# The opening of a two-layer hybrid backbone kernel: conditioning by row tiles, first blocks in passes, and a new order of three queues

## The chip, the core and the metric

The kernel runs on one core of a Trainium2 chip. The metric is the device time of the kernel in microseconds (us), as the median of several runs; less is better. PE is the tensor engine, DVE the vector engine, ACT the scalar engine, POOL the GpSimd engine, and SP the engine whose queue issues the loads.

## The reference

Two layers of a backbone run over 640 tokens: 128 context tokens (prompt) and 512 latent tokens (sample), width 1024. What the opening of the kernel computes is the first steps of layer 0, cut here to what matters:

```python
def _rmsnorm(x, g):
    y = xf * lax.rsqrt(jnp.mean(xf * xf, axis=-1, keepdims=True) + EPS)
    return (y * g.astype(jnp.float32)).astype(x.dtype)

def _modulation(cond, ada_w, ada_b):
    m = jax.nn.silu(cond) @ ada_w + ada_b
    return jnp.split(m[:, None, :], 6, axis=-1)
...
    sh1, sc1, ga1, sh2, sc2, ga2 = _modulation(cond, ada_w, ada_b)
    h = _rmsnorm(x, g_pre_mix) * (1.0 + sc1) + sh1
    mixed, side = mixer(_split_proj(h, w_in))
    x = x + ga1 * _rmsnorm(mixed @ w_out, g_post_mix)
    h = _rmsnorm(x, g_pre_ffn) * (1.0 + sc2) + sh2
    x = x + ga2 * _rmsnorm(_conv_ffn(h, w_up, conv_w, conv_b, w_down), g_post_ffn)
```

There are two conditioning rows: one for the context, one for the sample. Before the first projection `h @ w_in` can start, the kernel needs the shift and scale of both (16 column groups of 128 of `ada_w`), the row scale of the norm, and the transposed tokens.

## The kernel before, in words

The tokens are five tiles of 128 (`NT = 5`; tile 0 is the context). Every large product is taken in three parts from operands split in a high and a low half: high by high, high by low, and low by high. The high half is an ACT copy (`split_hi` and `lead_high`), the low half a DVE subtraction (`split_lo` and `lead_low`). Weights come through four slots of `raw` in an order fixed by tables; each engine has its own queue, written out by hand, and semaphores tie the queues together.

The opening is written apart from the loops over the layers. It has these pieces:

- Conditioning. SP loads the two rows of 1024 numbers as one row `cond_row` (L550). PE spreads it to all partitions with four products of a 1-partition column of ones, 512 columns each, into banks 0 to 3 (L2481). ACT takes the silu of each bank (L770). The first two make the row of the context, `cond[:, 0]`, the other two the row of the sample, `cond[:, 1]`.
- Modulation columns. SP loads 16 column groups of `ada_w` into the eight buffers of `lead`, first eight (half 0: groups 8, 0, 9, 1, 10, 2, 11, 3) and then eight more (half 1: groups 12, 4, 13, 5, 14, 6, 15, 7) into the buffers that come free. Five of them are done by PE (`lead_columns`, L2120: 0 to 2 are groups 0, 1, 2, then groups 4 and 5), eleven by DVE (`lead_products`, L1743 and L1746, one instruction for each conditioning row: 0 to 4 belong to half 0, 5 to 10 to half 1). `lead_mod(h)` on DVE finishes half h.
- Norm. For each tile ACT takes the squares and the root (`lead_squares`, L783 and L785), DVE the reciprocal (`row_scale`, L1388), ACT the scaled tokens `xl` (`lead_scaled`, L1041).
- Tokens by half. `lead_transposes(h, tt)` on PE (L2131) transposes four of the eight column groups of tile tt; a modulation by DVE (L1780) or ACT (L1051) writes `tf`, ACT copies the high half `aT_hi` (L1061), DVE makes `aT_lo` (L1787).
- First block. `lead_block(h, tt)` on PE takes the 12 products of tile tt with half h of the first 512 output columns: two weight granules (q), two k each, three products for each k (`mm3`, L2087 to L2089). It begins with a wait for `aT_lo` of its tile. The blocks run in order (0,0) to (0,4) and (1,0) to (1,4); after them the loops over the layers begin.

The queue of each engine around this:

```python
            for tt in range(NT):
                lead_block(0, tt)
                if tt < 2:
                    lead_columns((3 + tt,))
                if tt + 2 < NT:
                    lead_transposes(0, tt + 2)
                else:
                    lead_transposes(1, tt + 2 - NT)
```

Of the kernel before, what the change touches and what calls it, by code (L numbers as in the profile page):

```python
# [24 lines left out]
P = 128  # L25
# [142 lines left out]
def build(nc, t):  # L168
    with ExitStack() as ctx:
# [84 lines left out]
        with ExitStack() as s:  # L254
            xn = sb("xn", [P, 2, D], F32, s)
            zt = sb("zt", [P, W], F32, s)
            sq = sb("sq", [P, D], F32, s)
            with ExitStack() as s2:
                tf = sb("tf", [P, 2, KD, P], F32, s2)
                lead = sb("lead", [P, KD, 1024], F32, s2)  # L260
                xl = sb("xl", [P, NT, D], F32, s2)
                cond_row = sb("cond_row", [1, 2 * D], F32, s2)
                ones = sb("ones", [1, P], F32, s2)
                cond_T = sb("cond_T", [P, KD, 2], F32, s2)
            with ExitStack() as s2:
                s_sum = sb("s_sum", [P, 3, HP, HZ], F32, s2)
            y_mix = sb("y_mix", [P, NT, W], F32, s)
            gb_mix = sb("gb_mix", [P, 2, D], F32, s)
            h_all = sb("h_all", [P, KD, TZ], F32, s)
# [175 lines left out]
        def in_bank(b, tt):  # L445
            return IN_BANKS[b][tt]
# [76 lines left out]
        def _(sp_):  # L523
# [26 lines left out]
            sp_.dma_start(cond_row[:], t["cond"]).then_inc(cond_in, 16)  # L550
# [214 lines left out]
        def _(act):  # L765
# [5 lines left out]
            act.wait_ge(primed, 1)  # L771

# [294 lines left out]
            lead_scaled(1)  # L1067
            lead_high(0, 0)
            split_hi(1, 0)
            lead_squares(2)  # L1070
# [278 lines left out]
        def _(dve):  # L1349
# [444 lines left out]
            row_scale(0, 1, 0)  # L1794
            lead_mod(0)
            lead_modulate(0, 0)
            split_lo(0, 0)
            lead_low(0, 0)
            lead_modulate(0, 1)
            split_lo(1, 0)  # L1800
            row_scale(0, 2, 0)
            lead_low(0, 1)
            lead_products(5)
            row_scale(0, 3, 0)
            lead_products(6)
            lead_products(7)
            lead_low(0, 2)
            row_scale(0, 4, 0)
            lead_products(8)
            lead_low(0, 3)  # L1810
            lead_products(9)
            lead_products(10)
            lead_low(0, 4)
# [270 lines left out]
        def _(pe):  # L2084
# [65 lines left out]
            def lead_block(h, tt):  # L2150

                pe.wait_ge(norm_lo, NT * h + tt + 1)
                for q in (2 * h, 2 * h + 1):
                    if tt == 0:
                        pe.wait_ge(*freed(stream_of(q), 0))
                    for kk in range(2):
                        k = 2 * q + kk
                        i_ = mm3(bank[in_bank(0, tt)][:], aT_hi[:, k, toks(tt)], aT_lo[:, k, toks(tt)],
                                 w_hi[:, q, kk * W:(kk + 1) * W], w_lo[:, q, kk * W:(kk + 1) * W],
                                 k == 0, k == KD - 1)  # L2160
                    if tt == NT - 1:
                        i_.then_inc(w_used, 1)
                if h and tt < NT - 1:
                    i_.then_inc(in_done, 1)
# [314 lines left out]
            pe.wait_ge(cond_in, 16)  # L2479
            for i in range(4):  # L2480
                pe.matmul(bank[i][:], ones[:], cond_row[:, i * W:(i + 1) * W], start=True, stop=True).then_inc(cond_rows, 1)  # L2481
# [3 lines left out]
            lead_transposes(0, 0)  # L2485
            lead_transposes(0, 1)
            for tt in range(NT):
                lead_block(0, tt)
                if tt < 2:
                    lead_columns((3 + tt,))  # L2490
                if tt + 2 < NT:
                    lead_transposes(0, tt + 2)
                else:
                    lead_transposes(1, tt + 2 - NT)
# [297 lines left out]
```

## Time and profile before

| what | value |
|---|---|
| median of 3 runs | 1602.45 us (1602.03 to 1604.36) |
| the profiled execution, first to last instruction (its span) | 1601.0 us |
| PE busy | 1575.8 us (98%) |
| DVE busy | 1275.6 us (80%) |
| ACT busy | 794.1 us (50%) |
| POOL busy | 379.2 us (24%) |
| PE's share of the chain that ended last | 84% |
| DVE's share of the chain that ended last | 7% |

The profile is of one execution. Its own time is given as its span, 1601.0 us; the runs' times also hold what lies before the first and after the last instruction, and the median is 1.45 us over the span. Busy time is the time in which an engine executed; the chain that ended last is followed back from the last instruction to whatever released each step.

### The profile page before, as it was taken

Reading aid. Unit: us, or ns where it says so; the run is one execution under the profiler, and the core shown is the slowest. Engines: PE = TensorE matmul, PEld = TensorE weight load, DVE = VectorE, ACT = ScalarE, POOL = GpSimd, SP = SyncE. Lnnn points to the kernel's source line nnn. Section 1 sums busy time; section 2 is a strip of 40 time slices with the busy share of each in tenths; the row PEclk is TensorE's granted clock in tenths of the full one; section 3 lists DMA queues with packets and bytes.
Section 4 is the critical chain, followed back from the end, with each engine's and each line's share of the span. In section 5 each row is a group of like instructions: output and inputs, shape, how many; then the busy total and the mean of one; then the engine's idle time right before and its main releaser. Section 6 shows DMA issues by size and latency. Waiting matters only on the chain.

```text
span 1601.0 us, 28310 instructions
## 1 busy us (share of the span) xinstructions
PE 1575.8 (98%) x9688; PEld 1389.2 (87%) x9688; DVE 1275.6 (80%) x2255; ACT 794.1 (50%) x1483; POOL 379.2 (24%) x302
## 2 busy tenths in 40 slices
PE   8999999999999999999999999999999999999998
PEld 6788898689999999888878889967899999998886
DVE  7876677968999999966669556987689999998575
ACT  5433235638655565533383323274766565563333
POOL 0031033001455455200000400700035455541000
PEclk9999999999999999999999999999999999999999
DMA  9343265361222222454414414736312222335451
GB/s 369 122 132 111 74 222 179 95 168 55 66 81 89 79 92 79 148 168 158 152 40 145 138 54 134 260 107 146 79 64 82 80 91 79 92 92 178 125 184 66
DMA packets 65494, 195.04 MB, mean 122 GB/s; under 512 B 15361, under 2 KB 16769, under 8 KB 65153
## 3 DMA queue, kind: packets, MB, share of 16 engines
q1 hardware_dynamic: 50114, 175.54, 35.1%
q10 hardware_dynamic: 15296, 18.39, 3.5%
q8 instruction: 53, 0.87, 0.3%
q14 instruction: 31, 0.25, 0.1%
HBM read 187.05 MB, written 6.85 MB: 121 GB/s over the span
## 4 chain that ended last, share of the span: by engine, by line
PE 84%; DVE 7%; issue 2%; ACT 2%; DMA 1%; ACTq 1%; DVEq 0%; SPq 0%
PE bank L2087 14%; PE bank L2088 13%; PE bank L2089 13%; PE bank L2597 10%; PE bank L2599 10%; PE bank L2598 10%; DMA raw<-in_stream 1%; PE bank L2393 1%; PE bank L2457 1%; PE bank L2455 1%; PE bank L2453 1%; PE bank L2380 1%; PE bank L2109 1%; DVE w_lo L1354 1%; PE bank L2277 1%
## 5 line engine op out<-in xcount | busy, mean ns | idle before, releaser
L778 ACT ACTIVATE w_hi<-raw 128x1024 fp32r<-128x1024 f32 (+1 forms) x120 | 123.1, 1029 | 389.0 <-PE bank L2089 325.1
L1354 DVE TENSOR_TENSOR w_lo<-raw,w_hi 128x1024 fp32r<-128x1024 f32 (+1 forms) x128 | 156.3, 1228 | 162.4 <-ACT w_hi L778 162.2
L2087 PE MATMUL bank<-w_hi,aT_lo 128*128 128x512 f32 x520 | 210.5, 405 | 2.1 <-DVE aT_lo L1787 2.0
L2088 PE MATMUL bank<-w_lo,aT_hi 128*128 128x512 f32 x520 | 206.0, 396 | 0.0
L2089 PE MATMUL bank<-w_hi,aT_hi 128*128 128x512 f32 x520 | 205.6, 395 | 0.0
L2597 PE MATMUL bank<-aT_hi,w_lo 128*128 128x322 f32 x640 | 199.8, 312 | 4.5 <-DVE u L1953 4.5
L2598 PE MATMUL bank<-aT_lo,w_hi 128*128 128x322 f32 x640 | 199.4, 312 | 0.0
L2599 PE MATMUL bank<-aT_hi,w_hi 128*128 128x322 f32 x640 | 198.6, 310 | 0.0
L1252 ACT ACTIVATE w_hi<-raw 128x512 fp32r<-128x512 f32 x200 | 117.8, 627 | 105.8 <-POOL raw L660 105.8
L2087 PE MATMUL bank<-w_hi,m_lo 128*128 128x512 f32 x400 | 158.5, 396 | 0.0
L2088 PE MATMUL bank<-w_lo,m_hi 128*128 128x512 f32 x400 | 157.3, 393 | 0.0
L2089 PE MATMUL bank<-w_hi,m_hi 128*128 128x512 f32 x400 | 157.2, 393 | 0.0
L1942 DVE TENSOR_TENSOR w_lo<-raw,w_hi 128x512 fp32r<-128x512 f32 x200 | 140.7, 734 | 0.0
L2597 PEld LDWEIGHTS bank<-aT_hi,w_lo 128*128 128x128 f32 x640 | 120.7, 189 | 6.0 <-DVE u L1953 5.0
L2598 PEld LDWEIGHTS bank<-aT_lo,w_hi 128*128 128x128 f32 x640 | 121.3, 190 | 0.0
L2599 PEld LDWEIGHTS bank<-aT_hi,w_hi 128*128 128x128 f32 x640 | 121.3, 190 | 0.0
L2087 PEld LDWEIGHTS bank<-w_hi,aT_lo 128*128 128x128 f32 x520 | 98.2, 189 | 26.5 <-DVE aT_lo L1787 3.4
L2089 PEld LDWEIGHTS bank<-w_hi,aT_hi 128*128 128x128 f32 x520 | 98.4, 189 | 23.3
L2088 PEld LDWEIGHTS bank<-w_lo,aT_hi 128*128 128x128 f32 x520 | 98.4, 189 | 20.8
L649 POOL TENSOR_TENSOR raw<-raw 128x512 f32<-128x512 f32 x40 | 52.6, 1316 | 258.6 <-DVE bank L1983 137.4
L639 POOL TENSOR_TENSOR bias<-bias,masks 128x192 f32<-128x192 f32 (+1 forms) x48 | 59.1, 1269 | 198.0 <-DMA bias<-in_bias 198.0
L2599 PE MATMUL bank<-s_hi,w_hi 128*128 128x322 f32 x320 | 99.8, 312 | 0.0
(287 smaller groups left out, 3865.9 us busy)
## 6 DMA issues: line engine op xcount, KB each, us to landing
raw<-in_stream SPq DMA_DIRECT2D x304, 512.0 KB, 3.6
lead<-in_lead SPq DMA_DIRECT2D x16, 512.0 KB, 10.6
bias<-in_bias ACTq DMA_DIRECT2D x8, 896.0 KB, 10.3
na_v<-vn ACTq DMA_DIRECT2D x2, 1280.0 KB, 5.6
x<-in_xs SPq DMA_DIRECT2D x4, 512.0 KB, 12.4
vt<-na_v ACTq DMA_DIRECT2D x16, 128.0 KB
gb_mix<-gates ACTq DMA_DIRECT2D x2, 1024.0 KB, 6.2
gb_ffn<-gates ACTq DMA_DIRECT2D x8, 256.0 KB, 4.5
```

The source lines that it names most:

```text
L639: i_ = pool.tensor_tensor(part, part, masks[:, m0 * CG:(m0 + n) * CG].rearrange("p (g c) -> p g c", c=CG).unsqueeze(2) .to_broadcast([P, n ...
L649: pool.tensor_tensor(g_, g_, a_, ALU.subtract).then_inc(t1_done, 1)
L778: act.activation(w_hi[:, g % 4, 0:n], raw[:, s % 4, 0:n], ACT.Copy).then_inc(hi_done, 1)
L1252: act.activation(block_of(w_hi, n), block_source(n, e), ACT.Copy).then_inc(blk_hi, 1)
L1354: dve.tensor_tensor(w_lo[:, g % 4, 0:n], raw[:, s % 4, 0:n], w_hi[:, g % 4, 0:n].bitcast(F32), ALU.subtract).then_inc(raw_free[s % 4], 1)
L1942: i_ = dve.tensor_tensor(block_of(w_lo, n), block_source(n, e), block_of(w_hi, n).bitcast(F32), ALU.subtract)
L2087: pe.matmul(out, ll, rh, start=start, stop=False)
L2088: pe.matmul(out, lh, rl, start=False, stop=False)
L2089: return pe.matmul(out, lh, rh, start=False, stop=stop)
L2597: pe.matmul(out, wl, rhs_hi[:, k, :], start=k == 0, stop=False)
L2598: pe.matmul(out, wh, rhs_lo[:, k, :], start=False, stop=False)
L2599: i_ = pe.matmul(out, wh, rhs_hi[:, k, :], start=False, stop=k == HP - 1)
```

## The change

It has four parts.

1. Conditioning: the row is loaded in four pieces of 512 numbers to partitions 0, 32, 64 and 96, by four loads in place of one. The four products take their ones and their row from these partitions, so each lies in rows of its own of the tensor engine's array. The column of ones is filled on all 128 partitions. ACT also takes one square root of a constant after the silus, which brings the load of the table for the root ahead of the first squares.
2. `lead_block` works in passes by operand: for each granule first the two products high by high, then the two with the low half of the weights, then the two with the low half of the tokens. Each pass waits for its own operand.
3. PE's order: the transposes of tile 1 come behind block (0, 0), the fourth modulation column behind them.
4. ACT's and DVE's order: `lead_scaled(1)` behind the split of weight granule 1; on DVE `row_scale(1)` behind the modulation of tile 0, `lead_products(5)` ahead of the modulation of tile 1, and the products after it each one place later than the low half of a tile.

```diff
-                cond_row = sb("cond_row", [1, 2 * D], F32, s2)
-                ones = sb("ones", [1, P], F32, s2)
+                cond_row = sb("cond_row", [P, W], F32, s2)
+                ones = sb("ones", [P, P], F32, s2)
...
-            sp_.dma_start(cond_row[:], t["cond"]).then_inc(cond_in, 16)
+            for i in range(4):
+                sp_.dma_start(cond_row[32 * i:32 * i + 1, :], t["cond"][:, i * W:(i + 1) * W]).then_inc(cond_in, 16)
...
             act.wait_ge(primed, 1)
+            act.activation(prime[:, 15:16], eps[:], ACT.Sqrt)
...
             split_hi(0, 0)
-            lead_scaled(1)
             lead_high(0, 0)
             split_hi(1, 0)
+            lead_scaled(1)
             lead_squares(2)
...
             lead_products(4)
-            row_scale(0, 1, 0)
             lead_mod(0)
             lead_modulate(0, 0)
+            row_scale(0, 1, 0)
             split_lo(0, 0)
             lead_low(0, 0)
-            lead_modulate(0, 1)
             split_lo(1, 0)
             row_scale(0, 2, 0)
+            lead_products(5)
+            lead_modulate(0, 1)
             lead_low(0, 1)
-            lead_products(5)
             row_scale(0, 3, 0)
             lead_products(6)
+            lead_low(0, 2)
             lead_products(7)
-            lead_low(0, 2)
             row_scale(0, 4, 0)
+            lead_low(0, 3)
             lead_products(8)
-            lead_low(0, 3)
             lead_products(9)
+            lead_low(0, 4)
             lead_products(10)
-            lead_low(0, 4)
             lead_mod(1)
...
             def lead_block(h, tt):

-                pe.wait_ge(norm_lo, NT * h + tt + 1)
+                out = bank[in_bank(0, tt)][:]
+                pe.wait_ge(norm_hi, NT * h + tt + 1)
                 for q in (2 * h, 2 * h + 1):
+                    if tt == 0:
+                        pe.wait_ge(hi_done, q + 1)
+                    for kk in range(2):
+                        k = 2 * q + kk
+                        pe.matmul(out, aT_hi[:, k, toks(tt)], w_hi[:, q, kk * W:(kk + 1) * W], start=k == 0, stop=False)
                     if tt == 0:
                         pe.wait_ge(*freed(stream_of(q), 0))
                     for kk in range(2):
                         k = 2 * q + kk
-                        i_ = mm3(bank[in_bank(0, tt)][:], aT_hi[:, k, toks(tt)], aT_lo[:, k, toks(tt)],
-                                 w_hi[:, q, kk * W:(kk + 1) * W], w_lo[:, q, kk * W:(kk + 1) * W],
-                                 k == 0, k == KD - 1)
+                        pe.matmul(out, aT_hi[:, k, toks(tt)], w_lo[:, q, kk * W:(kk + 1) * W], start=False, stop=False)
+                    pe.wait_ge(norm_lo, NT * h + tt + 1)
+                    i_ = low_pass(tt, q)
...
-            pe.wait_ge(cond_in, 16)
+            pe.wait_ge(cond_in, 64)
             for i in range(4):
-                pe.matmul(bank[i][:], ones[:], cond_row[:, i * W:(i + 1) * W], start=True, stop=True).then_inc(cond_rows, 1)
+                row = slice(32 * i, 32 * i + 1)
+                pe.matmul(bank[i][:], ones[row, :], cond_row[row, :], start=True, stop=True).then_inc(cond_rows, 1)
             pe.wait_ge(cond_silu, 1)
             lead_columns(range(3))
             pe.wait_ge(ident_in, 16)
             lead_transposes(0, 0)
+            lead_block(0, 0)
             lead_transposes(0, 1)
-            for tt in range(NT):
+            lead_columns((3,))
+            lead_transposes(0, 2)
+            lead_block(0, 1)
+            lead_columns((4,))
+            lead_transposes(0, 3)
+            for tt in range(2, NT):
                 lead_block(0, tt)
-                if tt < 2:
-                    lead_columns((3 + tt,))
-                if tt + 2 < NT:
-                    lead_transposes(0, tt + 2)
-                else:
-                    lead_transposes(1, tt + 2 - NT)
+                lead_transposes(*divmod(tt + 2, NT))
```

ACT's queue from the scaled tokens of tile 0 on, before (`sq` and `std` are the squares and root of the next tile, `xl` its scaled tokens, `w_hi` a weight granule, `aT_hi` the high half of a tile):

```order
L1041 ACTIVATE xl<-x,rstd 128x1024
L783 ACTIVATE sq,ssq<-x 128x1024
L785 ACTIVATE std<-ssq,eps 128x1
L778 ACTIVATE w_hi<-raw 128x1024
L1041 ACTIVATE xl<-x,rstd 128x1024
L1061 ACTIVATE aT_hi<-tf 128x4x128
L778 ACTIVATE w_hi<-raw 128x1024
L783 ACTIVATE sq,ssq<-x 128x1024
L785 ACTIVATE std<-ssq,eps 128x1
L1061 ACTIVATE aT_hi<-tf 128x4x128
L1041 ACTIVATE xl<-x,rstd 128x1024
```

and in the changed kernel:

```order
L1043 ACTIVATE xl<-x,rstd 128x1024
L785 ACTIVATE sq,ssq<-x 128x1024
L787 ACTIVATE std<-ssq,eps 128x1
L780 ACTIVATE w_hi<-raw 128x1024
L1063 ACTIVATE aT_hi<-tf 128x4x128
L780 ACTIVATE w_hi<-raw 128x1024
L1043 ACTIVATE xl<-x,rstd 128x1024
L785 ACTIVATE sq,ssq<-x 128x1024
L787 ACTIVATE std<-ssq,eps 128x1
L1063 ACTIVATE aT_hi<-tf 128x4x128
L1043 ACTIVATE xl<-x,rstd 128x1024
```

The scaled tokens of tile 1 have moved two places down; the high half of tile 1 (`aT_hi`, second of the piece) still stands ahead of the scaled tokens of tile 2 (last row).

DVE's queue from the modulation of tile 0 on, before (`tf` from bank 3 is tile 0, from bank 6 tile 1; `rstd` is the reciprocal of a tile):

```order
L1780 TENSOR_SCALAR tf<-bank3,mod 128x128 x3
L1354 TENSOR_TENSOR w_lo<-raw,w_hi 128x1024 [waits hi_done]
L1787 TENSOR_TENSOR aT_lo<-tf,aT_hi 128x4x128 [waits norm_hi]
L1780 TENSOR_SCALAR tf<-bank6,mod 128x128 [waits mod_done,norm_tp]
L1780 TENSOR_SCALAR tf<-bank6,mod 128x128 x3
L1354 TENSOR_TENSOR w_lo<-raw,w_hi 128x1024 [waits hi_done]
L1388 RECIPROCAL rstd<-std 128x1 [waits pre_std]
L1787 TENSOR_TENSOR aT_lo<-tf,aT_hi 128x4x128 [waits norm_hi]
L1743 ISA ada_sq,mod<-lead,cond 128x1024 [waits cond_silu,ada_part,lead_full0]
```

and in the changed kernel:

```order
L1782 TENSOR_SCALAR tf<-bank3,mod 128x128 x3
L1390 RECIPROCAL rstd<-std 128x1 [waits pre_std]
L1356 TENSOR_TENSOR w_lo<-raw,w_hi 128x1024 [waits hi_done]
L1789 TENSOR_TENSOR aT_lo<-tf,aT_hi 128x4x128 [waits norm_hi]
L1356 TENSOR_TENSOR w_lo<-raw,w_hi 128x1024 [waits hi_done]
L1390 RECIPROCAL rstd<-std 128x1 [waits pre_std]
L1745 ISA ada_sq,mod<-lead,cond 128x1024 [waits cond_silu,ada_part,lead_full0]
L1748 ISA lead,mod<-lead,cond 128x1024 [waits cond_silu]
L1782 TENSOR_SCALAR tf<-bank6,mod 128x128 [waits mod_done,norm_tp]
L1782 TENSOR_SCALAR tf<-bank6,mod 128x128 x3
L1789 TENSOR_TENSOR aT_lo<-tf,aT_hi 128x4x128 [waits norm_hi]
L1390 RECIPROCAL rstd<-std 128x1 [waits pre_std]
```

The modulation of tile 1 (`tf` from bank 6) now stands behind a product (L1745 and L1748), and the reciprocals of tiles 1 and 2 stand on both sides of the weights' low halves.

PE's queue from the transposes of tile 0 to block (0, 1), in the changed kernel (bank 3 and bank 6 take transposes, bank 7 the modulation columns, bank 0 block (0, 0), bank 4 block (0, 1)):

```order
L2133 MATMUL bank3<-ident,xl 128x128 x4
L2161 MATMUL bank0<-w_hi,aT_hi 128x512 x2
L2166 MATMUL bank0<-w_lo,aT_hi 128x512 x2
L2148 MATMUL bank0<-w_hi,aT_lo 128x512 x2
L2161 MATMUL bank0<-w_hi,aT_hi 128x512 x2
L2166 MATMUL bank0<-w_lo,aT_hi 128x512 x2
L2148 MATMUL bank0<-w_hi,aT_lo 128x512 x2
L2133 MATMUL bank6<-ident,xl 128x128 x4
L2122 MATMUL bank7<-cond_T,lead 128x2 x8
L2133 MATMUL bank3<-ident,xl 128x128 x4
L2161 MATMUL bank4<-w_hi,aT_hi 128x512 x2
```

Before, the transposes into bank 6 stood directly behind those into bank 3, ahead of block (0, 0).

## Rows read from the trace of the kernel before

**Rows 1.** Head of the page.

```profile
span 1601.0 us, 28310 instructions
```

**Rows 2.** Chain that ended last, 44 to 50 us: start us, us, what.

```profile
44.19 1.14 DVE lead L1746
...
45.33 0.60 DVE aT_lo L1787
...
46.47 1.36 DVE tf L1780 x4
...
49.62 0.50 PE bank L2087
```

**Rows 3.** Timeline of PE, opening: start us, us, what, [idle before <- releaser].

```profile
2.48 7.16 PE L2481 MATMUL bank<-cond_row,ones 1*128 1x512 f32 x8 [2.48 <-DMA cond_row<-in_cond]
9.57 10.40 PE L2120 MATMUL bank<-cond_T,lead 128*128 128x2 f32 x48
19.83 1.09 PE L2131 MATMUL bank<-ident,xl 128*128 128x128 f32 x4
...
24.96 0.80 PE L2087 MATMUL bank<-w_hi,aT_lo 128*128 128x512 f32 x1 [0.77 <-DVE aT_lo L1787]
...
30.25 2.10 PE L2120 MATMUL bank<-cond_T,lead 128*128 128x2 f32 x16
...
32.61 0.47 PE L2087 MATMUL bank<-w_hi,aT_lo 128*128 128x512 f32 x1
...
35.48 1.84 PE L2120 MATMUL bank<-cond_T,lead 128*128 128x2 f32 x16
```

**Rows 4.** SP's queue: timeline to 1.5 us; loads of half 0's second and seventh columns.

```profile
0.75 0.35 SPq L550 DMA_DIRECT2D cond_row<-in_cond  x1
1.16 0.37 SPq L551 DMA_DIRECT2D cond_T<-in_cond_T  x1
...
L531 SPq DMA_DIRECT2D lead<-in_lead x1: 432/432/432, 2.0 to 2.0; - x1
...
DMA to landing us min/median/max: 4.7/4.7/4.7
...
L531 SPq DMA_DIRECT2D lead<-in_lead x1: 652/652/652, 5.6 to 5.6; - x1
...
DMA to landing us min/median/max: 9.3/9.3/9.3
```

**Rows 5.** Timeline of DVE, opening.

```profile
16.04 1.22 DVE L1743 CUSTOM_DVE_ANT_0 ada_sq<-lead,cond 128x1024 f32<-128x1024 f32 x1
...
21.07 0.16 DVE L1388 RECIPROCAL rstd<-std 128x1 f32<-128x1 f32 x1 [0.31 <-ACT std L785]
...
21.81 1.37 DVE L1780 TENSOR_SCALAR tf<-bank,mod 128x128 f32<-128x128 f32 x4
...
37.50 0.16 DVE L1388 RECIPROCAL rstd<-std 128x1 f32<-128x1 f32 x1 [1.71 <-ACT std L785]
```

**Rows 6.** Timeline of ACT, opening.

```profile
26.22 0.63 ACT L1061 ACTIVATE aT_hi<-tf 128x512 fp32r<-128x512 f32 x1
27.43 1.15 ACT L1041 ACTIVATE xl<-x,rstd 128x1024 f32<-128x1024 f32 x1 [0.57 <-DVE rstd L1388]
...
29.65 0.30 ACT L785 ACTIVATE std<-ssq,eps 128x1 f32<-128x1 f32 x1
32.89 1.50 ACT L1051 ACTIVATE tf<-bank,mod 128x128 f32<-128x128 f32 x4 [2.94 <-PE bank L2131]
```

**Rows 7.** PE waits over the span (total, times, longest); PE by stretches: PEclk is the granted clock.

```profile
PE bank L2597 <- DVE u L1953: 4.5, 2, 2.3
...
432.00:434.00 2.00, 2.00 (x15) 1.00 0.48 182
...
1212.00:1214.00 2.00, 2.00 (x7) 0.50 0.54 213
1214.00:1216.00 2.00, 2.00 (x11) 0.70 0.00 0
```

## Prediction

> **What bounds the kernel now.** The first view is the head of the page: the execution profiled took 1601.0 us [rows 1]. The median of the runs is 1602.45 us, 1.45 us more; I make the sum on the profiled execution and add 1.45. About 0.2% (3.2 us) is what a measurement of this kernel can tell from no change.
>
> The second view is the chain that ended last. From 49.62 us on it runs through PE with next to no gap, and just before it runs through DVE: a product for a modulation column, the low half of tile 4, `lead_mod(1)`, the modulation of tile 0 in half 1 at 46.47, a weight's low half and the tile's low half, then PE's block (1,0) [rows 2]. So everything after block (1,0) is PE's work; the opening counts only by the moment at which PE can enter block (1,0) and does not stop again. That moment is set by DVE's queue.
>
> The third view is the timelines of the opening. PE does the conditioning products from 2.48 to 9.6, three columns to 19.97, transposes, and block (0,0) from 24.96 to 30.25: 12 products in 5.3 us, 0.44 each. Block (0,1) takes 32.61 to 35.48, 0.24 each [rows 3]. So PE ran at its lower clock (1.2 GHz) up to about 30 us and at 2.4 GHz after, though the profile prints a granted clock of 1.00 for both. DVE has hardly a gap: it waits 0.31 us ahead of the reciprocal of tile 1 and 1.71 us ahead of that of tile 4 [rows 5].
>
> **The change, part by part.**
>
> *Four loads for one.* A load of the row holds SP's queue for 0.41 us (0.75 to 1.16) [rows 4]. Three more put every later load 1.2 us back. The loads are in a row that DMA works off without a pause, so the landings should move by as much: bounds 0 (the backlog absorbs it) and 1.2; I take 1.2, since the whole backlog starts later. The column for DVE's fourth product landed at 5.6 + 9.3 = 14.9 us [rows 4] and DVE started on it at 16.04 [rows 5]. It will land at 16.1.
>
> *Row-tiled products.* Four products take 7.16 us now, 1.8 each [rows 3]. Each in rows of its own, they can lie over one another: bounds are 1.8 us (full overlap) and 7.2 (none). I take near full overlap: they start at 3.7 (2.48 + 1.2) and end at about 5.7, against 9.6 now. None of this arrives. DVE's fourth product waits for its column until 16.1, against 16.04 before, so the reciprocal of tile 0, its scaled tokens and PE's transposes stay at 19.8. PE has room too: its three columns need 10.4 us [rows 3] and, begun at 7.9 when the second column lands (2.0 + 4.7 [rows 4] + 1.2), end at 18.4. The Trainium skill (TensorE: Matmul & The Clock Gate, Part 3) gives a speedup of 3.07 for four row tiles of 512 columns; by an estimate from it the products would take 2.3 us. The same page and TensorEngine Tiling (Key Properties) speak against the change as well: switching the tiling mode drains the engine. No row here shows either, and both would leave the sum as it is, as the room of 1.4 us hides them.
>
> *The early table load.* ACT loads the root's table before the tokens land instead of after; the root of tile 0 is wanted only at 18.3. Cost and gain nothing, and if the cover went it would be one short table load.
>
> *Tile 0 first.* DVE no longer waits 0.31 us for the root of tile 1 and does not take its reciprocal: the modulation of tile 0 starts at 21.4 instead of 21.81 [rows 5] and ends at 22.75. ACT takes the high half at once (0.63 [rows 6]), and PE can start block (0,0) with high by high at 23.45, not 24.96: 1.5 us earlier. At the same lower clock, 12 x 0.43 = 5.1 us, it ends at 28.6 instead of 30.25. This is the gain of the change.
>
> *What it delays.* Tile 1 has moved back on all three engines.
> - ACT: high half of tile 0 to 23.4, weight granule 1 (about 1.0) and only then `xl` of tile 1, from 24.3 to 25.4. From the start of an `xl` to the root of the next tile it is 2.5 us (27.43 to 29.95 [rows 6]), so the root of tile 2 is there at 26.8. DVE is done with two weight granules (1.14 each, taken like a product of as many columns) and a low half (0.6) [rows 2] at 25.7, waits 1.1 to 1.2 us for that root, and then does the product, to 29.2.
> - PE transposes tile 1 behind the block: 28.6 + 1.1 [rows 3] = 29.7. DVE modulates it from 29.7 to 31.1, ACT copies the high half to 31.7 (26.85 before [rows 6]).
> - ACT's queue is in order, so `xl` of tile 2 is written from 31.7 to 32.8 (27.43 before), and the root of tile 3 is ready 2.5 us after its start, at 34.2 (29.95 before): 4.2 us later [rows 6]. DVE stands before its reciprocal from 32.4 to 34.2: 1.8 us idle, with a product queued behind it that needs nothing.
> - PE's transposes of tile 2 wait for that `xl` until 32.8, so block (0,1) starts at 33.3 against 32.61, and the transposes of tile 3 come at 37.9 (33.3 + 2.9 + 1.7).
> - DVE from 34.2: two products of 2.3 (two instructions of 1.14 each [rows 2]), a low half of 0.6 and reciprocals to 39.6; then it waits 1.2 us for the high half of tile 3 (37.9 + 0.5 transposes + 1.5 modulation [rows 6] + 0.6 high half + hand-over = 40.8). Then low half, two products, low half, product, `lead_mod`: 0.6 + 4.6 + 0.6 + 2.3 + 0.6 = 8.7, to 49.5.
>
> So the modulation of half 1, tile 0, starts at 49.5 against 46.47: 3.05 us late. A check by idle time: DVE's waits grow from 2.0 (0.31 + 1.71) to 5.4 (1.2, 0.5 before the modulation of tile 1, 0.7 for its high half, 1.8, 1.2), its work is the same, so 3.4, less the 0.4 above.
>
> *Passes by operand.* Block (1,0) now starts on the high half, not on the low one. The high half is ready at 49.5 + 1.4 + 0.6 = 51.5, so PE enters at 51.6 against 49.62, 2.0 us late; the low half comes at 52.7, and granule 3's low half at 53.9, which leaves the block's end at 54.8 against about 52.65: 2.15 late. The later blocks gain the 0.2 us for which block (1,4) waited. The number of products and weight loads is the same, so nothing else moves.
>
> **Sum.** 2.15 - 0.2 = +2.0 us: span 1603.0, run 1604.4 us. Bounds of the terms: landings not delayed, -1.2; the full clock reached during block (0,0), -0.5; silus and columns late, +1.1 (below).
>
> **The rivals.**
>
> *Slower: the clock falls in the new gap.* PE finishes block (0,4) and its transposes at 49.0 and then stands idle to 51.6, 2.6 us. In the loops, PE has two idle stretches of 2.2 to 2.3 us for the same reason (DVE's `u`). After the one near 430 us the clock stayed whole (15 products in 2 us); after the one that ended at 1212 us it was 0.50 and then 0.70, with 7 and 11 products in 2 us [rows 7]. Against 15.5, 13 products are missing at 0.13 us: 1.7 us. If it happens here, where PE is the bound from then on, the time is 1604.4 + 1.7 = 1606.1, slower by 0.23%. It decides from about 2.2 us of idle; for it speaks that the new gap is longer than both, against it that one of two was spared. Chance 0.32. The Trainium skill (TensorE: Matmul & The Clock Gate, Why this matters for your kernels) warns only of idle stretches longer than this one; by that rule the sum stays at 1604.4. The trace has a shorter one that cost the clock, so I go by the trace.
>
> *The row tiles don't overlap.* Then PE's columns start at 10.9 and end at 21.3, past the 19.7 at which `xl` of tile 0 is there, and tile 0 comes 1.4 us late; some is hidden by DVE's later waits: +1.1, 1605.5. Against it: separate rows and banks. Chance 0.08.
>
> *The delay is smaller.* Landings as before and the clock up early: 2.0 - 1.2 - 0.5 = +0.3, 1602.75. It needs both bounds; chance 0.15.
>
> *A real gain*, which needs DVE's waits to stay as they were: chance 0.03, 1 to 3 us.
>
> **How the numbers follow.** Forecast 0.42: 1604.4. Slower by over 0.2% is above 1605.65: most of the clock case (0.25), half of the overlap case and a tail of the forecast, together 0.30. Faster by over 0.2% would need more than all that DVE and PE wait in the opening: 0.03. Same: 0.67. The runs of before alone lie 2.3 us apart. The range takes in the small case less 1 us and the clock case plus 0.9: 1601.8 to 1607.0.
>
> **What would show it.** Right: column landings 1.2 us later; block (0,0) at 23.5; an ACT gap ahead of tile 1's high half of over 4 us; DVE idle 1.8 us ahead of tile 3's reciprocal; block (1,0) at 51.6. Clock case: products of 0.43 us apart after it. Wrong: block (1,0) before 49.6, or DVE without gaps between 25 and 41 us.

## The result, and the profile after

| | before | changed |
|---|---|---|
| median, measured side by side | 1602.94 us (9 runs, 1601.29 to 1606.08) | 1607.06 us (9 runs, 1604.46 to 1609.12) |
| ratio to before | | 1.0021, 95% interval 1.0013 to 1.0029 |
| span of the profiled execution | 1601.0 us | 1605.2 us |
| mean granted clock over the runs | 0.9975 (33 runs of a later measurement; 0.9973 to 0.9976 in all four) | 0.9958 |

The changed kernel is slower by about 0.2%; the interval leaves out 1. A second measurement (below) gave 1.0035 with 1.0022 to 1.0048.

The timeline of PE in the changed kernel, opening (columns as in [rows 3]; "x2" is one pass of two products of 512 columns):

```profile
3.18 2.09 PE L2490 MATMUL bank<-cond_row,ones 1*128 1x512 f32 x8 [3.18 <-DMA cond_row<-in_cond]
7.66 10.37 PE L2122 MATMUL bank<-cond_T,lead 128*128 128x2 f32 x48 [2.40 <-DMA lead<-in_lead]
19.25 1.09 PE L2133 MATMUL bank<-ident,xl 128*128 128x128 f32 x4 [1.21 <-ACT xl L1043]
22.94 1.22 PE L2161 MATMUL bank<-w_hi,aT_hi 128*128 128x512 f32 x2 [2.61 <-ACT aT_hi L1063]
...
32.16 1.11 PE L2133 MATMUL bank<-ident,xl 128*128 128x128 f32 x4 [1.49 <-ACT xl L1043]
32.92 1.20 PE L2161 MATMUL bank<-w_hi,aT_hi 128*128 128x512 f32 x2
...
36.92 1.84 PE L2122 MATMUL bank<-cond_T,lead 128*128 128x2 f32 x16
...
52.41 1.21 PE L2161 MATMUL bank<-w_hi,aT_hi 128*128 128x512 f32 x2 [2.40 <-ACT aT_hi L1063]
53.42 1.05 PE L2166 MATMUL bank<-w_lo,aT_hi 128*128 128x512 f32 x2
...
56.86 0.60 PE L2133 MATMUL bank<-ident,xl 128*128 128x128 f32 x4
```

The first row is the row-tiled conditioning, 2.09 us where [rows 3] have 7.16; PE then idles 2.40 us, since the column is not there. Block (0,0) starts 2.0 us earlier than before, but block (1,0) 2.79 us later (52.41 against 49.62) and behind an idle stretch of 2.40 us.

PE leaves block (1,0) at 56.86 in the changed kernel, when the next transposes begin. Before, these stand at

```profile
52.48 0.60 PE L2131 MATMUL bank<-ident,xl 128*128 128x128 f32 x4
```

So 4.38 us are lost by then, 2.79 ahead of the block and 1.59 in it, and that covers the whole difference of the two spans (1605.2 less 1601.0): what follows takes 1548.3 us in the changed kernel and 1548.5 before.

The timeline of DVE, the rows with a wait and the modulations of tile 0 (20.86), tile 1 (29.03) and half 1 (50.33):

```profile
15.46 1.22 DVE L1745 CUSTOM_DVE_ANT_0 ada_sq<-lead,cond 128x1024 f32<-128x1024 f32 x1 [0.18 <-DMA lead<-in_lead]
...
20.86 1.37 DVE L1782 TENSOR_SCALAR tf<-bank,mod 128x128 f32<-128x128 f32 x4
...
26.27 0.17 DVE L1390 RECIPROCAL rstd<-std 128x1 f32<-128x1 f32 x1 [1.12 <-ACT std L787]
...
29.03 1.37 DVE L1782 TENSOR_SCALAR tf<-bank,mod 128x128 f32<-128x128 f32 x4 [0.23 <-PE bank L2133]
31.09 0.69 DVE L1789 TENSOR_TENSOR aT_lo<-tf,aT_hi 128x512 fp32r<-128x512 f32 x1 [0.70 <-ACT aT_hi L1063]
33.51 0.17 DVE L1390 RECIPROCAL rstd<-std 128x1 f32<-128x1 f32 x1 [1.72 <-ACT std L787]
...
41.51 0.69 DVE L1789 TENSOR_TENSOR aT_lo<-tf,aT_hi 128x512 fp32r<-128x512 f32 x1 [2.51 <-ACT aT_hi L1063]
...
50.33 1.36 DVE L1782 TENSOR_SCALAR tf<-bank,mod 128x128 f32<-128x128 f32 x4
```

DVE waits 6.3 us between 20 and 50 us. Before, it was 2.2: the 0.31 and 1.71 of [rows 5] and 0.17 for a high half. ACT's timeline shows where the wait of 1.72 us begins: the high half of tile 1 holds the queue until DVE has modulated the tile, and the scaled tokens of tile 2 and the root of tile 3 stand behind it.

```profile
30.43 0.63 ACT L1063 ACTIVATE aT_hi<-tf 128x512 fp32r<-128x512 f32 x1 [4.19 <-DVE tf L1782]
30.97 1.14 ACT L1043 ACTIVATE xl<-x,rstd 128x1024 f32<-128x1024 f32 x1
...
33.18 0.30 ACT L787 ACTIVATE std<-ssq,eps 128x1 f32<-128x1 f32 x1
```

In [rows 6] these stand at 26.22, 27.43 and 29.65. PE by stretches (us, PE busy and products, granted clock, DMA share, GB/s):

```profile
30.00:32.00 2.00, 0.67 (x7) 0.99 1.04 414
32.00:34.00 2.00, 1.84 (x7) 0.50 1.02 401
34.00:36.00 2.00, 2.00 (x7) 0.65 1.02 408
36.00:38.00 2.00, 2.00 (x16) 1.00 1.02 394
...
50.00:52.00 2.00, 0.01 (x1) 1.00 0.00 0
52.00:54.00 2.00, 1.59 (x4) 0.61 0.17 10
54.00:56.00 2.00, 2.00 (x7) 0.53 0.78 248
56.00:58.00 2.00, 2.00 (x12) 1.00 0.80 213
```

The granted clock falls to 0.50, which is 1.2 GHz, twice: behind the stretch in which PE worked 0.67 of 2 us and idled 1.49 ahead of 32.16, in block (0,1), and behind the gap of 2.40 us, in block (1,0). Before, it fell neither there nor elsewhere in the opening once it was up. In the same stretch before, block (1,0) ran at the whole clock:

```profile
50.00:52.00 2.00, 2.00 (x10) 1.00 0.86 250
52.00:54.00 2.00, 2.00 (x12) 1.00 0.79 213
```

### The profile page after: what moved, and what is told of

Read it like the earlier page. It is cut to its first block, busy times and chain, and to the rows that moved or that the text cites. A ratio compares the mean times of both kernels' runs of the same rounds, so it can differ in the third digit from the quotient of the medians.

```text
span 1605.2 us, 28314 instructions
## 1 busy us (share of the span) xinstructions
PE 1573.2 (98%) x9688; PEld 1389.3 (87%) x9688; DVE 1276.5 (80%) x2255; ACT 793.7 (49%) x1484; POOL 378.2 (24%) x302
## 4 chain that ended last, share of the span: by engine, by line
PE 84%; DVE 7%; issue 2%; ACT 2%; DMA 1%; ACTq 0%; DVEq 0%; SPq 0%
PE bank L2089 13%; PE bank L2090 13%; PE bank L2091 13%; PE bank L2607 10%; PE bank L2609 10%; PE bank L2608 10%; DMA raw<-in_stream 1%; PE bank L2401 1%; PE bank L2465 1%; PE bank L2463 1%; PE bank L2461 1%; DVE ada_sq L1367 1%; PE bank L2388 1%; PE bank L2111 1%; DVE w_lo L1356 1%
## 5 line engine op out<-in xcount | busy, mean ns | idle before, releaser
L2089 PE MATMUL bank<-w_hi,aT_lo 128*128 128x512 f32 x480 | 192.8, 402 | 0.0
L2090 PE MATMUL bank<-w_lo,aT_hi 128*128 128x512 f32 x480 | 189.3, 394 | 0.0
L2091 PE MATMUL bank<-w_hi,aT_hi 128*128 128x512 f32 x480 | 188.9, 394 | 0.0
L2091 PEld LDWEIGHTS bank<-w_hi,aT_hi 128*128 128x128 f32 x480 | 90.3, 188 | 21.3
L2089 PEld LDWEIGHTS bank<-w_hi,aT_lo 128*128 128x128 f32 x480 | 90.2, 188 | 21.5 <-issue 1.0
L2090 PEld LDWEIGHTS bank<-w_lo,aT_hi 128*128 128x128 f32 x480 | 90.3, 188 | 19.4
```

Of the source, the lines that this page charges most:

```text
L2089: pe.matmul(out, ll, rh, start=start, stop=False)
L2090: pe.matmul(out, lh, rl, start=False, stop=False)
L2091: return pe.matmul(out, lh, rh, start=False, stop=stop)
```

## The experiments

Each ratio is to the kernel before, measured on the same chip beside it, with its 95% interval. The quotient of the two medians can differ from it by up to 0.0012. "Block (1,0)" is the moment at which PE enters it, in the profiled execution; "DVE waits" is its waiting between 20 and 50 us (to 51.0 and 51.5 in the two marked *, where the modulation of half 1 comes later). Kernels are listed by ratio. By an estimate from these figures, a fall of 0.0017 in the mean granted clock is 2.7 us of 1603.

| kernel | ratio | block (1,0), us | DVE waits, us | mean granted clock |
|---|---|---|---|---|
| passes alone | 0.9976 (0.9967 to 0.9985) | 46.94 | 0.3 | 0.9980 |
| parts 1 and 2 | 0.998 (0.9971 to 0.9989) | 46.33 | 0.3 | 0.9979 |
| part 1 alone | 0.9993 (0.9984 to 1.0002) | 48.96 | 1.3 | 0.9975 |
| parts 1, 2, ACT's order | 0.9996 (0.9987 to 1.0005) | 48.98 | 2.4 | 0.9980 |
| parts 1, 2, DVE's order, two calls exchanged | 0.9996 (0.9987 to 1.0005) | 49.23 | 3.0 | 0.9980 |
| before | 1 | 49.62 | 2.2 | 0.9973 to 0.9976 |
| changed, root of tile 3 first | 1.0003 (0.9994 to 1.0012) | 49.32 | 3.3 | 0.9972 |
| the same, and PE's gap filled | 1.0005 (0.9996 to 1.0014) | 49.16 | 3.3 | 0.9977 |
| changed, PE's old order | 1.0011 (1.0002 to 1.002) | 50.60 | 4.5 | 0.9974 |
| new orders of my own | 1.0016 (1.0006 to 1.0025) | 50.59 | 4.1 | 0.9961 |
| changed, PE's gap filled * | 1.0019 (1.001 to 1.0028) | 53.10 | 6.1 | 0.9973 |
| changed, first measurement | 1.0021 (1.0013 to 1.0029) | 52.41 | 6.3 | 0.9958 |
| parts 1, 2, DVE's order | 1.0025 (1.0014 to 1.0035) | 52.29 | 5.9 | 0.9958 |
| changed, second measurement * | 1.0035 (1.0022 to 1.0048) | 53.56 | 7.1 | 0.9948 |

One profile can't show what a kernel's clock does on the whole. In the loops over the layers, at about 430 and 1210 us, each kernel here has the same two idle stretches of PE, 2.23 to 2.29 us ([rows 7] show them before). Over the 14 profiles the products behind them ran at the lower clock in 14 of the 28 cases. With the root first, for one, it was

```profile
1212.00:1214.00 2.00, 1.39 (x5) 0.61 0.86 260
```

and with the root first and the gap filled, where PE's loops are the same,

```profile
1212.00:1214.00 2.00, 1.94 (x13) 1.00 0.56 219
```

Such a loss costs about 1.5 us (12 products missing in 4 us, of 0.13 each, from the counts before), so profiled spans differ by up to 3 us for this alone. The table's moments in the opening come from one profile each; the ratios and the mean clocks come from all runs.

**Part 1 alone.** Before, with the four loads, the row tiles and the early table load.

> The kernel before with part 1 alone: four loads, row-tiled products, the early table load; all orders and blocks as before. Order theory (part 1 is harmless, the loss lies in the new orders): the loads land 0.3 to 0.6 us later, but DVE's fourth product starts at 15.5 instead of 16.04, so everything behind it comes about 0.5 us sooner: 0.5 us faster than before, block (1,0) at about 49.1. Landing theory (the later landings are what costs): DVE and PE get later by the shift, 0.3 to 1.2 us slower than before.

Measured 0.9993 (0.9984 to 1.0002): no change that can be told. The products take 2.09 us, and PE's columns end at 18.7 us; `xl` of tile 0 is what PE waits for next (1.48 us ahead of its transposes at 20.14, which stand at 19.83 in [rows 3]). So the 5 us that the conditioning gives back (7.16 less 2.09) end in waits for loads: in this kernel DVE waits 0.76 and 1.65 us for its second and third column.

**Parts 1 and 2.** The passes by operand too, the three old orders kept.

> Parts 1 and 2 of the change with the three old orders. Order theory: block (1,0) starts on the high half and no wait of 0.2 us is left ahead of block (1,4), so another 0.6 us is won over part 1 alone: 1.1 us faster than before in all, 5 us faster than the changed kernel. Passes theory (the grouping of the products itself slows PE): at or above the time of before, with products more than 0.235 us apart inside a block.

Measured 0.998 (0.9971 to 0.9989), 3.2 us faster than before and more than the 1.1 expected. The interval leaves out 1. Block (1,0) starts at 46.33 us, and DVE has no wait but the 0.31 us for the root of tile 1.

**Passes alone.** Before, with only `lead_block` changed as in the diff:

```diff
             def lead_block(h, tt):
-                pe.wait_ge(norm_lo, NT * h + tt + 1)
+                pe.wait_ge(norm_hi, NT * h + tt + 1)
...
```

> The kernel before with the passes by operand alone. Order theory: each block starts on its high half, so PE's waits of 1.0, 0.2 and 0.5 us ahead of blocks (0,4), (1,4) and (0,0) shrink or go: 1 to 2.5 us faster than before, most of what parts 1 and 2 together gave (3.2). Rival (the two parts only work together, as the row tiles start DVE sooner): within 0.5 us of before.

Measured 0.9976 (0.9967 to 0.9985): 3.8 us faster, more than the 1 to 2.5 expected. It needs only part 2; from parts 1 and 2 together (0.998) it can't be told. DVE no longer waits for the root of tile 4 (1.71 us in [rows 5]): its timeline runs

```profile
35.05 0.69 DVE L1787 TENSOR_TENSOR aT_lo<-tf,aT_hi 128x512 fp32r<-128x512 f32 x1
35.86 0.16 DVE L1388 RECIPROCAL rstd<-std 128x1 f32<-128x1 f32 x1
36.01 1.23 DVE L1743 CUSTOM_DVE_ANT_0 ada_sq<-lead,cond 128x1024 f32<-128x1024 f32 x1
...
44.86 1.37 DVE L1780 TENSOR_SCALAR tf<-bank,mod 128x128 f32<-128x128 f32 x4
```

and PE, whose blocks no longer wait for the low half, writes its transposes 1.6 us earlier:

```profile
24.11 1.22 PE L2159 MATMUL bank<-w_hi,aT_hi 128*128 128x512 f32 x2
...
30.96 0.74 PE L2159 MATMUL bank<-w_hi,aT_hi 128*128 128x512 f32 x2
...
46.94 0.74 PE L2159 MATMUL bank<-w_hi,aT_hi 128*128 128x512 f32 x2
```

Block (0,1) stands at 30.96 against 32.61 and block (1,0) at 46.94 against 49.62. The gain is a loop closed over three engines: an earlier block gives earlier transposes, those an earlier modulation and high half on ACT, an earlier root, and DVE's one large wait is gone. In the profile block (1,0) ends at 50.19 us, 2.3 us sooner than before; the 3.8 us of the ratio have an interval of 2.4 to 5.3. The profiled span is only 0.8 us shorter than before (1600.2), since the clock fell behind both idle stretches of the loops here and behind one of them before.

**The root first.** The changed kernel; on ACT the scaled tokens of tile 2 and the root of tile 3 go ahead of the high half of tile 1:

```diff
-            lead_high(0, 1)
             lead_scaled(2)
             lead_squares(3)
+            lead_high(0, 1)
```

> The changed kernel with one move on ACT: the scaled tokens of tile 2 and the squares and root of tile 3 ahead of the high half of tile 1. Order theory: DVE's wait of 1.7 us ahead of tile 3's reciprocal and PE's 1.5 us ahead of tile 2's transposes go; the first loss of clock goes with them, and block (1,0) comes 1.5 to 2 us sooner: 2 us faster than the changed kernel, still 2 us slower than before. Rival (that wait hides behind the later one for the high half of tile 3): within 0.5 us of the changed kernel.

Measured 1.0003 (0.9994 to 1.0012), 2.9 us less than the changed kernel's 1.0021, as the order theory had it. The wait of 1.72 us is gone, that for the high half of tile 3 is 1.48 us instead of 2.51:

```profile
26.41 0.17 DVE L1392 RECIPROCAL rstd<-std 128x1 f32<-128x1 f32 x1 [1.12 <-ACT std L787]
...
38.41 0.69 DVE L1791 TENSOR_TENSOR aT_lo<-tf,aT_hi 128x512 fp32r<-128x512 f32 x1 [1.48 <-ACT aT_hi L1063]
...
47.24 1.37 DVE L1784 TENSOR_SCALAR tf<-bank,mod 128x128 f32<-128x128 f32 x4
```

So the place of the high half of tile 1, at the head of ACT's queue, carries some 3 us of the slip (50.33 to 47.24), with the fall of the clock in block (0,1), which the profile no longer has. Moving it gives back the slowdown within the interval, though not the gain of the passes.

**The gap filled.** The changed kernel with 12 needless products of 512 columns behind the transposes of block (1,0), and block (0,4) behind them, so that PE does not stand still ahead of block (1,0). Their results are written over by block (0,4).

```diff
-            for tt in range(2, NT):
-                lead_block(0, tt)
-                lead_transposes(*divmod(tt + 2, NT))
...
+            lead_transposes(1, 0)
+            fill(12)
+            lead_transposes(1, 1)
+            lead_block(0, 4)
```

> The changed kernel with 12 needless products on PE ahead of the transposes of tile 1, half 1 and block (0,4), which overwrites them; they fill most of PE's idle 2.4 us ahead of block (1,0) and change no other queue. Clock theory: the clock stays at 2.4 GHz, block (1,0) starts at the same 52.4 but its products are 0.23 apart instead of 0.43: 1.5 us faster than the changed kernel. Rival (the clock costs nothing, the slip alone does): the same time as the changed kernel within 0.5 us, though nothing is computed with the 12.

Measured 1.0019 (1.001 to 1.0028), mean granted clock 0.9973. Block (1,0) is now run at the whole clock:

```profile
46.92 3.03 PE L2491 MATMUL bank<-w_hi,aT_hi 128*128 128x512 f32 x12
...
53.10 0.74 PE L2161 MATMUL bank<-w_hi,aT_hi 128*128 128x512 f32 x2
53.68 0.62 PE L2166 MATMUL bank<-w_lo,aT_hi 128*128 128x512 f32 x2
...
56.35 0.60 PE L2133 MATMUL bank<-ident,xl 128*128 128x128 f32 x4
```

The block takes 3.25 us (53.10 to 56.35) against 4.45 (52.41 to 56.86) in the changed kernel: the clock cost it 1.2 us. The same block takes 3.24 us in the three kernels here that enter it behind the gap and keep the clock (root first, PE's old order, calls exchanged). From the first transposes to block (1,0) it is 32.9 us (20.18 to 53.10), as in the changed kernel (19.25 to 52.41, 33.2), so the filling delays nothing. But the ratio lies only at the lower one of the changed kernel's two (1.0021 and 1.0035); the quotient of the medians is 1.0011. That the clock is given back rests on the mean over 11 runs (0.9973 against 0.9958 and 0.9948) more than on the one profile. How much of the time is given back is not settled.

**PE's old order.** The changed kernel with PE's queue as before.

> The changed kernel with PE's old order (tile 1's transposes ahead of block (0,0)), ACT's and DVE's orders as changed. Queue theory (ACT's and DVE's orders make the loss): block (0,0) loses its early start, the waits ahead of the roots stay, the time stays within 1 us of the changed kernel. PE theory (the transposes behind the block make the loss): 3 us faster than the changed kernel, near the kernel before.

Measured 1.0011 (1.0002 to 1.002), clock 0.9974. This lies between the two expectations: 1.6 us under the first measurement of the changed kernel and 3.8 under the second. DVE waits 1.12, 0.70, 1.72 and 1.04 us, so most of the waiting is there without the transposes behind the block; what the old order changes in the profile is that PE keeps its clock through block (0,1) and that the wait for the high half of tile 3 is 1.04 and not 2.51.

**New orders of my own.** Parts 1 and 2, and orders of the three queues meant to shorten every wait at once: the low halves later on DVE, the root first, column 5 behind block (0,3).

> Parts 1 and 2 with three new orders: on ACT the scaled tokens, squares and roots of tiles 2 and 3 stand ahead of the high halves of the tiles before them, on DVE the products 6 to 10 stand in pairs between reciprocals and low halves, on PE the fifth modulation column goes behind block (0,3). Order theory: no engine stands before a root, DVE is never idle from 20 to 48 us, block (1,0) starts at about 46 us: 4 to 6 us faster than before and 1 to 2.5 us faster than parts 1 and 2 with the old orders. Rival (the opening is at the floor that the loads set): the same as those.

Measured 1.0016 (1.0006 to 1.0025): a miss by 6 us and more, and neither theory held. DVE's `lead_mod(1)` waits for the fifth column:

```profile
47.56 0.16 DVE L1775 TENSOR_TENSOR mod<-bank,par 128x4 f32<-128x4 f32 x1 [2.94 <-PE bank L2126]
```

and PE stops inside two blocks for the low halves that now stand behind products:

```profile
36.25 1.01 PE L2152 MATMUL bank<-w_hi,aT_lo 128*128 128x512 f32 x2 [2.16 <-DVE aT_lo L1791]
...
43.72 0.73 PE L2152 MATMUL bank<-w_hi,aT_lo 128*128 128x512 f32 x2 [1.99 <-DVE aT_lo L1791]
```

**The changed kernel again**, to measure its spread.

> The changed kernel once more, as the measure for the others of this chip: 1.002 of the kernel before. Clock theory: its mean granted clock over the runs is below that of the kernel before by 0.0015 or more, since PE idles in two more places for long enough to lose it. Slip theory (the loss is all in the order): the same mean clock as before.

Measured 1.0035 (1.0022 to 1.0048, five runs), clock 0.9948; in its profile block (1,0) starts at 53.56 us. The two intervals of the same kernel meet only between 1.0022 and 1.0029, so each ratio of this table holds to about 0.001 and not better.

**One queue at a time.** To the kernel with parts 1 and 2 (0.998) I added ACT's new order alone, then DVE's alone.

```diff
             split_hi(0, 0)
-            lead_scaled(1)
             lead_high(0, 0)
             split_hi(1, 0)
+            lead_scaled(1)
```

> Parts 1 and 2 of the change with PE's and DVE's order of before; only ACT's queue as in the change: the scaled tokens of tile 1 behind weight granule 1. With both old orders the kernel stood at 0.998 of before, with ACT's and DVE's new order under PE's old one at 1.0011: 5 us lie in those two queues. Theory (they lie in DVE's queue, by the product ahead of the modulation of tile 1): this kernel stays near 0.998 to 0.999, DVE without a wait of over 1 us between 28 and 45 us, block (1,0) entered by 47.5 us. Rival (they lie in ACT's queue, because the root of tile 2 comes behind a weight granule more): 1.000 to 1.001, DVE waiting over 1 us for the root of tile 2, block (1,0) at 48.5 us or later.

Measured 0.9996 (0.9987 to 1.0005), between the two expectations; its interval meets that of parts 1 and 2 (0.9971 to 0.9989). Block (1,0) starts at 48.98 us. The wait is not the one that either named: tile 1's scaled tokens are late, so PE transposes them late (it idles 4.98 us ahead of them) and DVE waits for the transposes.

```profile
27.32 1.37 DVE L1784 TENSOR_SCALAR tf<-bank,mod 128x128 f32<-128x128 f32 x4 [2.12 <-PE bank L2135]
```

> Parts 1 and 2 of the change with PE's and ACT's order of before; only DVE's queue as in the change: the product of a column stands ahead of the modulation of tile 1, and reciprocal 1 behind the modulation of tile 0. Theory (the 5 us lie in DVE's queue): 1.000 to 1.001; the high half of tile 1 is 2.3 us late, with it the scaled tokens of tile 2 and the root of tile 3, for which DVE waits 1.5 us or more; block (1,0) entered at 48.5 us or later. Rival (they lie in ACT's queue): 0.998 to 0.999 and block (1,0) by 47.5 us.

Measured 1.0025 (1.0014 to 1.0035): DVE's order alone costs 0.0045 over the kernel without it, 7 us, as much as all three orders together. Its timeline has the waits of the changed kernel, though PE's and ACT's queues are the old ones:

```profile
33.32 0.17 DVE L1390 RECIPROCAL rstd<-std 128x1 f32<-128x1 f32 x1 [1.72 <-ACT std L787]
...
41.39 0.69 DVE L1789 TENSOR_TENSOR aT_lo<-tf,aT_hi 128x512 fp32r<-128x512 f32 x1 [2.57 <-ACT aT_hi L1063]
...
50.21 1.37 DVE L1782 TENSOR_SCALAR tf<-bank,mod 128x128 f32<-128x128 f32 x4
```

**Two calls exchanged.** The same kernel with one line moved:

```diff
-            lead_products(5)
             lead_modulate(0, 1)
+            lead_products(5)
             lead_low(0, 1)
```

> The kernel with only DVE's new order (1.0025 of before) with two of its calls exchanged: the modulation of tile 1 again ahead of the product of a column, everything else of DVE's new order kept. Theory (the one exchange is the cost, since the high half of tile 1, the scaled tokens of tile 2 and the root of tile 3 hang on it): 0.998 to 0.999 of before, DVE's wait for the root of tile 3 under 0.5 us instead of 1.72, that for the high half of tile 3 under 1 us instead of 2.57, block (1,0) entered by 47.5 us. Rival (the cost lies in the later places of the products or of the reciprocal of tile 1): 1.000 or more, block (1,0) after 48.5 us.

Measured 0.9996 (0.9987 to 1.0005). The one exchange gives back 0.0029, 4.6 us, and with it the mean granted clock (0.9980 after 0.9958); block (1,0) starts 3.06 us earlier. The wait for the root of tile 3 falls from 1.72 to 0.22 us:

```profile
30.98 0.17 DVE L1390 RECIPROCAL rstd<-std 128x1 f32<-128x1 f32 x1 [0.22 <-ACT std L787]
...
38.32 0.69 DVE L1789 TENSOR_TENSOR aT_lo<-tf,aT_hi 128x512 fp32r<-128x512 f32 x1 [1.84 <-ACT aT_hi L1063]
```

It does not reach 0.998: a wait of 1.84 us for the high half of tile 3 stays, and block (1,0) starts at 49.23 us, not by 47.5. By the timeline it belongs to the other half of DVE's new order, the low half of tile 3 ahead of product 8: DVE comes to it 1.8 us before it can be had, with the product that would fill the time behind it. So both theories hold a part: some two thirds of the cost of DVE's order lie in the exchange. That the rest lies in the later products, and not in the later reciprocal of tile 1, is argued and no run separates the two.

**Both remedies.** The root first and the gap filled.

> The changed kernel with both remedies: ACT takes the scaled tokens of tile 2 and the root of tile 3 ahead of the high halves of tiles 0 and 1, and PE fills its gap ahead of block (1,0) with 12 needless products. If the late root and the lost clock are two separate costs, each removes its own: 0.998 to 0.9995 of before and a mean granted clock of 0.9975 or more. If they are one and the same (the gap ahead of block (1,0) closes by either), the filling adds nothing to 1.0003 or costs the time of products that stand in the way: 1.0003 to 1.001.

Measured 1.0005 (0.9996 to 1.0014), clock 0.9977. The filling adds nothing to the root first (1.0003). Block (1,0) is entered at 49.16 us, as with the root first alone (49.32), where the gap of 2.40 us had not cost the clock in the profile: there was little to win back. So of the two expectations the second held.

## Why the prediction was right, and where not

The sum gave +2.0 us and, if the clock fell in the new gap, +3.7; measured were +4.1 us as a difference of medians, 1.0021 as a ratio (3.4 us), and 1.0035 in the second measurement. The direction is that of the forecast, and so is the slip but for 0.8 us (block (1,0) entered at 52.41 and not at 51.6); the time is that of the rival. The two terms that were missing, 0.8 of entry and 1.2 of clock in block (1,0), make up all but 0.2 of the difference between +2.0 and the 4.2 of the spans.

- *Four loads.* SP's queue shows 1.22 us for the four and the first column's load at 2.42 instead of 1.58. I took 1.2 us for every landing. The load of the column for DVE's fourth product is issued at 6.3 and takes 9.1 to land, 15.4 against 14.9; the landing moved by 0.5. DVE started on its fourth product at 15.46, not at 16.1, and 0.6 us earlier than before, not level. The term was too large. Nothing came of it: the modulation of tile 0 at 20.86 instead of 21.4 went into the later waits.
- *Row-tiled products.* Right: 2.09 us, taken as 2.0, and PE's columns ended at 18.03 (18.4). The four run over one another. The Trainium skill (TensorE: Matmul & The Clock Gate, Part 3) states 3.07 for four row tiles of 512 columns; 7.16 to 2.09 is 3.4. This case agrees in the main, with one partition of data in each tile. The drain at a switch of the tiling mode, which the prediction puts to two pages of the Trainium skill, stands in one of them (TensorEngine Tiling, Key Properties) and not in the other; it can't be seen here, since PE idles 2.40 us at the switch.
- *The early table load.* Right, no cost and no gain that shows: behind it ACT still idles 2.62 us until the tokens land. No run has it alone.
- *Tile 0 first.* Block (0,0) at 22.94 (23.45) and over at 28.23 (28.6): the gain of the change, and right.
- *What it delays.* The list of waits was right in place and nearly in size: 1.12 (1.2), 0.23 (0.5), 0.70 (0.7), 1.72 (1.8). **The step that failed is the last, "it waits 1.2 us for the high half of tile 3": it was 2.51.** DVE came to it some 0.6 us sooner than I had it, the tile 0.7 us later. I had block (0,1) at the whole clock, 2.9 us; it took 4.0 (32.92 to 36.92), at a granted clock that had fallen to 0.50 behind PE's idle stretch of 1.49 us. So tile 3 was transposed at 38.63 and not at 37.9, and the modulation of half 1 came at 50.33 instead of 49.5.
- *The clock in the new gap.* I gave it 0.32; it fell, in both profiles of the changed kernel, and cost 1.2 us in block (1,0) (4.45 against 3.25 us). That is less than the 1.7 of the rival, but the first fall, which I had not listed, adds its part. Of four other kernels with such a gap (2.40 to 2.42 us: root first, PE's old order, calls exchanged, DVE's order alone) it fell in the profile of the last only. That the case decides from about 2.2 us of idle, as the prediction says, is not borne out: 1.49 us ahead of block (0,1) went with a fall, 2.40 three times with none. Over the runs, the mean granted clock is 0.0017 lower than before, 2.7 us by the estimate above; the part in block (0,1) is already in the slip.
- *Passes by operand.* I costed them only as the entry of block (1,0), with nothing else moved. Alone, in the old orders, they are worth 3.8 us. I set them against the new orders only, where their effect on the earlier blocks is lost in the slip, and never asked what they would do to the old ones, whose one large wait, 1.71 us for the root of tile 4, they remove. What they are worth inside the changed kernel no run tells, since none takes them out of it.

So the parts are: passes, -3.2 us (with part 1); ACT's order on top of them +2.6 (0.9996 against 0.998, intervals that meet); DVE's order on top of them +7.2 (1.0025). They do not add: with both under PE's old order the kernel is at 1.0011, less than with DVE's order alone. The difference, 0.0014, is no more than the two measurements of the changed kernel lie apart, and the mean clocks differ by as much (0.9974 against 0.9958), so no cause is claimed for it.

Shown by a run: that the slip comes from DVE's queue and by way of ACT's (the exchange, the root first), and that the changed kernel has its clock back when the gap is filled. Not shown: that the gap alone costs the clock, since three kernels have the gap and keep it. Only argued: what costs the clock of block (0,1). The four profiles in which it fell there (the changed kernel twice, the gap filled, DVE's order alone) have ahead of it a modulation column, products of two elements a row, and then 0.65 to 2.42 us of idle time; before, PE went from the column to the block without a stop and kept it.

## What to carry to other kernels

Where three engines feed one another through queues in order, a step that needs nothing (a product of a column) put ahead of a step that others wait for can cost more than its length: here 2.3 us of product moved the entry of block (1,0) by 3.06 us and the time by 4.6, a part of it by the clock. Count for each step moved who waits on the far side, and keep steps without inputs as filling behind the ones that release others. Undo the parts one by one: here a change that was slower as a whole held one part, the passes by operand, that alone beats both kernels. And compare mean clocks over many runs before reading a few microseconds out of one profile.

## What the hardware showed that I had not expected

- An idle stretch of 2.4 us on PE cost the clock in some profiles and not in others, as the 2.23 to 2.29 us of the loops did (14 of 28). The granted clock fell behind it in both profiles of the changed kernel (2.40, 2.42) and with DVE's order alone (2.42), and stayed whole in three other kernels (2.40 to 2.41). Where it fell, it had also fallen some 20 us earlier; whether that is a cause is open. In my own orders it fell behind 2.16 us (0.63 and 0.52 from 36 to 40 us) and held behind 1.99 us at 43.72. The Trainium skill (TensorE: Matmul & The Clock Gate, Why this matters for your kernels) warns of longer stretches only; the traces do not bear that out as a safe bound.
- PE's work before block (0,0), the columns of two elements a row, filled it for 10.4 us, and the products behind it still ran at half the later rate. Before, the transposes follow the columns without a gap and take 1.09 us ([rows 3]), against 0.60 for four such transposes from 44 us on. In every kernel block (0,0) begins so (in those with passes, 1.05 us a pass against 0.62 later) and gets faster within it or right behind it. The rows print a granted clock of 1.00 all the while, so up to 30 us the rate has to be read from the products.
- The four row tiles take 2.09 us together, though each has only one partition of 32-bit data. They end about together: ACT's first silu starts at 5.26, just when the group ends (3.18 and 2.09), and the four silus follow without a gap.
